# The attention of a two-layer block, one head at a time and two heads at a time

## The reference, cut to what matters

```python
qa, ka = rope(rms_norm(qa)), rope(rms_norm(ka))    # 4 heads of 64
qb, kb = rope(rms_norm(qb)), rope(rms_norm(kb))    # 8 heads of 64 on 2 of k and v
qc, kc = rope(rms_norm(qc)), rope(rms_norm(kc))    # 4 heads, each 2 halves of 32
ya = softmax(causal(qa @ ka.T * 64**-0.5)) @ va
yb = softmax_with_sink(window(qb @ kb.T * 64**-0.5)) @ vb
p = softmax(causal(qc @ kc.T * 32**-0.5))          # for both halves
yc = rms_norm((p[0] - lam * p[1]) @ vc) * (1 - lam_init)
merged = g0 * (ya @ w_pa) + g1 * (yb @ w_pb) + g2 * (yc @ w_pc)
x = x + merged @ w_out
```

## Time and profile before

| | |
|---|---|
| median of 3 runs | 2590.4 us (2590.0 to 2590.89) |
| span of the profiled execution | 2589.5 us |
| PE busy | 2536.0 us, 98% |
| DVE busy | 1838.2 us, 71% |
| ACT busy | 1304.3 us, 50% |
| POOL busy | 116.2 us, 4% |
| DMA, mean over the span | 215 GB/s |

### The profile page before, as it was taken

One profiled execution on the slowest core, in us unless ns is written; L12 is line 12 of the kernel. 1 busy time (PEld: TensorE's weight loads), 2 busy tenths in 40 slices (PEclk: granted clock), 3 DMA queues, 4 the chain that ended last, 5 costly groups with the idle time before them and its releaser, 6 DMA issues.

```text
span 2589.5 us, 41592 instructions
## 1 busy us (share of the span) xinstructions
PE 2536.0 (98%) x16522; PEld 2192.0 (85%) x16522; DVE 1838.2 (71%) x2257; ACT 1304.3 (50%) x1535; POOL 116.2 (4%) x125
## 2 busy tenths in 40 slices
PE   8999999999999999999999999999999999999997
PEld 7888999888999988789989887788888888888886
DVE  6647767855777565375554843698898888988988
ACT  5554545453544421234334212377677677777765
POOL 1100000300000011100000110000000000000000
PEclk9999999999999999999999999899999999999998
DMA  5344553423555331136544212489989999999995
GB/s 213 140 183 159 183 181 145 144 97 134 212 180 195 131 131 66 66 147 235 182 151 164 106 66 98 171 332 357 353 339 354 344 347 358 348 349 344 352 353 211
DMA packets 77326, 558.21 MB, mean 216 GB/s; under 512 B 8704, under 2 KB 8960, under 8 KB 9856
## 3 DMA queue, kind: packets, MB, share of 16 engines
q1 hardware_dynamic: 76320, 550.93, 57.4%
q0 software_dynamic: 864, 5.24, 0.5%
HBM read 555.09 MB, written 1.05 MB: 215 GB/s over the span
## 4 chain that ended last, share of the span: by engine, by line
PE 91%; DVE 4%; ACT 2%; issue 2%; DMA 0%; DVEq 0%; ACTq 0%; SPq 0%; POOL 0%
PE bank L648 23%; PE bank L1137 18%; PE bank L1162 10%; PE bank L638 9%; PE bank L677 7%; PE bank L709 4%; PE bank L729 3%; PE bank L662 2%; PE bank L1110 1%; DVE w_lo L2489 1%; PE bank L1147 1%; PE bank L956 1%; PE bank L970 1%; PE bank L967 1%; ACT w_hi L1645 1%
## 5 line engine op out<-in xcount | busy, mean ns | idle before, releaser
L2489 DVE TENSOR_TENSOR w_lo<-ring,w_hi 128x2048 fp32r<-128x2048 f32 x216 | 486.2, 2288 | 54.1 <-ACT w_hi L1645 53.0
L1645 ACT ACTIVATE w_hi<-ring 128x2048 fp32r<-128x2048 f32 x216 | 404.9, 1916 | 20.6 <-PE bank L1137 17.0
L1137 PE MATMUL bank<-w_hi,xe_hi 128*128 128x512 f32 x792 | 311.4, 393 | 1.1
L1137 PE MATMUL bank<-w_hi,xe_lo 128*128 128x512 f32 x792 | 308.7, 390 | 0.0
L1137 PE MATMUL bank<-w_lo,xe_hi 128*128 128x512 f32 x792 | 308.5, 390 | 0.0
L648 PE MATMUL bank<-x_hi,w_hi 128*128 128x256 f32 x1008 | 285.3, 283 | 0.0
L648 PE MATMUL bank<-x_hi,w_lo 128*128 128x256 f32 x1008 | 285.2, 283 | 0.0
L648 PE MATMUL bank<-x_lo,w_hi 128*128 128x256 f32 x1008 | 285.2, 283 | 0.0
L1740 DVE TENSOR_TENSOR w_lo<-ring,w_hi 128x2048 fp32r<-128x2048 f32 x97 | 222.1, 2290 | 86.5 <-ACT w_hi L1266 84.4
L638 PE MATMUL bank<-xT,ring 128*128 128x256 f32 x1088 | 253.8, 385 | 1.1 <-ACT Z L1554 1.1
L1266 ACT ACTIVATE w_hi<-ring 128x2048 fp32r<-128x2048 f32 x99 | 189.4, 1913 | 109.4 <-PE bank L677 71.4
(11 more groups left out here) (371 smaller groups left out, 5127.4 us busy)
## 6 DMA issues: line engine op xcount, KB each, us to landing
ring<-in_stream SPq DMA_DIRECT2D x431, 1024.0 KB, 5.1
yT<-in_stream SPq DMA_DIRECT2D x54, 1024.0 KB, 6.9
xT<-in_stream SPq DMA_DIRECT2D x27, 1024.0 KB, 7.1
Z<-in_stream SPq DMA_DIRECT2D x8, 1024.0 KB, 8.1
norm_rows<-in_rows POOLq DMA_DIRECT2D x4, 1024.0 KB, 8.5
par<-in_par SPq DMA_DIRECT2D x1, 1335.0 KB, 9.6
cst<-in_cst SPq DMA_DIRECT2D x1, 1216.0 KB, 13.3
xres<-in_x SPq DMA_DIRECT2D x2, 512.0 KB, 4.1
```

Source lines behind the costliest of these rows:

```text
L1137: r = mm(banks[4 + j % 2], a[:, k, :], moe_part(b, i)[:, q * 512:(q + 1) * 512], start=(k == 0 and a is xe_hi and b is w_hi), stop=(k == K ...
L1645: act_(moe_part(w_hi, at), moe_slot(at), ACT.Copy).then_inc(*A.done("moe_hi", at))
L2489: v.tensor_tensor(moe_part(w_lo, at), moe_slot(at), moe_part(w_hi, at).bitcast(F32), ALU.subtract)\
```

## The change

Two jobs of `JOBS` make a pair, and a step now takes a pair: 10 pairs and 13 steps. The two heads of a pair of a or b lie in partitions 0 to 63 and 64 to 127 of q and k; for c the pair is c0 and c1 of one head, in neighbouring 32 partitions. The steps stand after the halves 18, 20, 21, 23, 25, 27, 28, 30, 32, 34, 35, 37 and 39:

```diff
+        PAIRS = [(JOBS[2 * t], JOBS[2 * t + 1]) for t in range(len(JOBS) // 2)]
+        N_PAIRS = len(PAIRS)
...
-            out, steps_left = [], list(range(len(JOBS) + 3))
-
-            def step():
-                if not steps_left:
+            out, steps_left = [], list(range(N_PAIRS + 3))
+
+            def step(halves_done):
+                t = N_PAIRS + 3 - len(steps_left)
+                if not steps_left or halves_done < (3 + 7 * (t - 1) // 4 if t else 1):
                     return
-                t = steps_left.pop(0)
-                if t < len(JOBS):
+                steps_left.pop(0)
+                if t < N_PAIRS:
                     out.append(("score", t))
-                if 1 <= t <= len(JOBS):
+                if 1 <= t <= N_PAIRS:
                     out.append(("norm", t - 1))
-                if 2 <= t <= len(JOBS) + 1:
+                if 2 <= t <= N_PAIRS + 1:
                     out.append(("turn", t - 2))
                 if 3 <= t:
                     out.append(("value", t - 3))
+                if not steps_left:
+                    out.append(("csquare", 0))
...
-                if k >= FIRST_STEP:
-                    step()
+                step(2 * (k - FIRST_STEP) + 1)
                 out.append(("half", 2 * k + 1))
-                if k >= FIRST_STEP:
-                    step()
+                step(2 * (k - FIRST_STEP) + 2)
```

The scores of a pair go to two banks, banks 0 and 1 for even pairs and banks 6 and 7 for odd ones; the latter are those of `sumsq` and `rotate`, so that score 1 waits for their last readers. The matmuls of the two heads alternate. The six transposes of a pair of a or b take bank 2 and 128 columns in each of the two banks of the pair scored a step before:

```diff
+                            if n >= 3 and br_pairs(n - 3):
+                                pe.wait_ge(*A.of("probT", l, n - 3))
+                        elif n == 1:
+                            pe.wait_ge(*A.of("qrms", l, len(QK_PAIRS) - 1))
+                            pe.wait_ge(*V.of("rotsin", l, len(QK_PAIRS) - 1))
+                        for late in range(2):
+                            for bank, (br, h, ot, ob, qt, kt, base, kk_, vc) in zip(score_banks(n), PAIRS[n]):
+                                q = qk[base:base + kk_, qt * SEQ:(qt + 1) * SEQ]
+                                k = qk[base:base + kk_, kt * SEQ:(kt + 1) * SEQ]
+                                if late:
+                                    mm(bank[:, 128:384], q[:, 128:256], k, start=True, stop=True).then_inc(*T.done("score", l, n))
+                                else:
+                                    mm(bank[:, 0:128], q[:, 0:128], k[:, 0:128], start=True, stop=True)
+                    elif kind == "turn":
...
+                            pe.wait_ge(*A.of("probT", l, n - 1))
+                        for j in ((0, 1) if br_pairs(n) else (1,)):
+                            for i in range(3):
+                                at = 3 * j + i if br_pairs(n) else i
+                                r = nc.tensor.transpose(banks[2][:, at * P:(at + 1) * P] if at < 4 else score_banks(n + 1)[at - 4][:, 384:512],
+                                                        prob[:, n % 3, j, cols3(i)], ct("ident"))
```

The values of two heads go to columns 0 to 63 and 64 to 127 of the array, alternating. For c the values of two pairs (two heads) are taken together, with the odd pair:

```diff
+                    elif kind == "value" and values_in(n):
...
+                        if n >= 1:
+                            pe.wait_ge(*A.of("y", l, PAIRS[n - 1][0][2] if br_pairs(n) else PAIRS[n][0][2] - 1))
+                        for late in range(2):
+                            for j in range(2):
+                                br, h, ot, ob, qt, kt, base, kk_, vc = PAIRS[n][j] if br_pairs(n) else PAIRS[n - 1 + j][1]
+                                dst, turned = banks[3][ob:ob + HD, 0:SEQ], probTs[turned_to(n)][:, j * 384:(j + 1) * 384]
+                                if late:
+                                    mm(dst[:, 128:256], vtm[:, 1, vc:vc + HD], turned[:, 256:384], start=False, stop=True)\
+                                        .then_inc(*T.done("value", l, n))
+                                else:
+                                    mm(dst, vtm[:, 0, vc:vc + HD], turned[:, 0:256], start=True, stop=False)
```

with `values_in(t)` giving `[t]` for a and b, and for c `[t - 1, t]` where t is odd, else nothing. So there are 10 scores, 10 turns (6 of six transposes, 4 of three) and 8 values. The mask's result is written to `prob` (three buffers of two heads), and the exponential works in place there; `msk` is gone. ACT:

```diff
+                        nm, rsm, se = sm(f"negmax{n % 2}", 4), sm(f"rowsum{n % 2}", 4), sm(f"sinkexp{n % 2}", 4)
+                        for j in range(2):
+                            for i, s in enumerate((slice(0, 128), slice(128, 384))):
+                                at = 2 * j + i
+                                act_(prob[:, n % 3, j, s], prob[:, n % 3, j, s], ACT.Exp, bias=nm[:, at:at + 1],
+                                     scale=scale, accum_out=rsm[:, at:at + 1]).then_inc(*A.done("exp", l, n))
...
+                        for u in turned_before(n):
+                            sc.wait_ge(*T.of("value", l, u))
+                        to = probTs[turned_to(n)]
+                        if br_pairs(n):
+                            act_(to[:, 0:512], banks[2], ACT.Copy).then_inc(*A.done("probT", l, n))
+                            for j in range(2):
+                                act_(to[:, (4 + j) * P:(5 + j) * P], score_banks(n + 1)[j][:, 384:512], ACT.Copy)\
+                                    .then_inc(*A.done("probT", l, n))
+                        else:
+                            act_(to[:, (n % 2) * 384:(n % 2 + 1) * 384], banks[2][:, 0:384], ACT.Copy).then_inc(*A.done("probT", l, n))
```

On DVE there are four masks in a row and one negative maximum of four columns; one reciprocal of four columns; and, for c, the first half is scaled by the same instruction as a and b and the second subtracted from it:

```diff
-                        if n >= 2:
-                            ve.wait_ge(*A.of("exp", l, n - 2))
-                            ve.wait_ge(*V.of("prob", l, n - 2))
-                        for i, s in enumerate((slice(0, 128), slice(128, 384))):
-                            v.tensor_tensor_reduce(out=msk[:, n % 2, s], in0=banks[n % 2][:, s], in1=mask[:, s], scale=1.0,
-                                                   scalar=-3.0e38, op0=ALU.add, op1=ALU.max,
-                                                   accum_out=sm("rowmax", 2)[:, i:i + 1]).then_inc(*V.done("masked", l, n))
+                        if n >= 3:
+                            ve.wait_ge(*T.of("turnp", l, n - 3))
+                        for j in range(2):
+                            for i, s in enumerate(blocks):
+                                v.tensor_tensor_reduce(out=prob[:, n % 3, j, s], in0=score_banks(n)[j][:, s], in1=mask[:, s], scale=1.0,
+                                                       scalar=-3.0e38, op0=ALU.add, op1=ALU.max,
+                                                       accum_out=sm("rowmax", 4)[:, 2 * j + i:2 * j + i + 1]).then_inc(*V.done("masked", l, n))
...
+                        if br[0] == "c":
+                            v.tensor_scalar(rsm[:, 2:4], rsm[:, 2:4], sm("neglam", 1), None, ALU.mult).then_inc(*V.done("rlam", l, n))
+                        for i, s in enumerate(blocks):
+                            v.tensor_scalar(prob[:, n % 3, 0, s], prob[:, n % 3, 0, s], rsm[:, i:i + 1], None, ALU.mult)\
+                                .then_inc(*V.done("prob", l, n))
+                        if br[0] == "c":
                             own()
-                        for i, s in enumerate((slice(0, 128), slice(128, 384))):
-                            pb = prob[:, n % 3, s]
-                            if br == "c1":
-                                v.scalar_tensor_tensor(out=pb, in0=pb, scalar=rsm[:, i:i + 1],
-                                                       in1=prob[:, (n - 1) % 3, s], op0=ALU.mult, op1=ALU.add)\
-                                    .then_inc(*V.done("prob", l, n))
+                        for i, s in enumerate(blocks):
+                            pb = prob[:, n % 3, 1, s]
+                            if br[0] == "c":
+                                v.scalar_tensor_tensor(out=pb, in0=pb, scalar=rsm[:, 2 + i:3 + i], in1=prob[:, n % 3, 0, s],
+                                                       op0=ALU.mult, op1=ALU.add).then_inc(*V.done("prob", l, n))
```

More of the change, by code:

```diff
@@ L397, in emit, with br_pairs, score_banks, turned_to @@
         SCHED = attention_schedule()
+        def br_pairs(t):
+            return PAIRS[t][0][0] in "ab"
+        def score_banks(t):
+            return (banks[0:2], banks[6:8])[t % 2]
+        def turned_to(t):
+            return t % 2 if br_pairs(t) else t // 2 % 2
+        def values_in(t):
+            return [t] if br_pairs(t) else [t - 1, t] if t % 2 else []
+        def turned_before(t):
+            own = t - t % 2 if not br_pairs(t) else t
+            return [u for u in range(own) if values_in(u) and turned_to(u) == turned_to(t)][-1:]
         class Filler:
@@ L1333, in unit @@
                         act_(squares[:, 8 * SEQ:9 * SEQ], bank[:, 0:SEQ], ACT.Square).then_inc(*A.done("square", l, 8))
-                        act_(msk[:, 0, 0:SEQ], bank[:, SEQ:2 * SEQ], ACT.Copy).then_inc(*A.done("in1", l, n))
+                        act_(vb_rows, bank[:, SEQ:2 * SEQ], ACT.Copy).then_inc(*A.done("in1", l, n))
                     elif n < 9:
@@ L1361, in block1 @@
                             .then_inc(*A.done("vb", l))
+                    if kind == "csquare":
+                        for i in range(2):
+                            sc.wait_ge(*A.of("y", l, 6 + i))
```

(27 more changed lines are left out.)

59 lines of the change are left out of this document (17 added, 42 removed).

## The result

The median went from 2590.89 us (2590.00 to 2591.32, five runs) to **2580.41 us** (2579.42 to 2580.95, five runs): ratio 0.9959, 95% interval 0.9947 to 0.9970, 10.5 us less. The profiled execution of the changed kernel has a span of 2579.1 us against 2589.5.

What follows compares the result with a forecast made beforehand. PE, busy 98% of the span, bounds the kernel; its 17.4 us saving per layer shrinks to 6.9 through waits. Less 3.4 for clock, over two layers, plus 1.5: 8.5 us gained, forecast 2582 us, range 2575 to 2589.

Steps and rivals of the forecast that it cites:

- Pairs at once: PE's scores and values: two heads run together at one head's price plus .03 us; PE saves 17.4 us per layer.
- Rival 2: Scores and values: pairs don't run at once in the array, each costing .60 us more; 2585 us, chance 0.15.
- Score 1's wait: At half 20, PE stands idle at score 1 until DVE's rotsin 6 ends; 5.8 us.
- The ring: After score 1, DVE and ACT's queued masks, exponentials, copies and splits set the pace; 9.1 us per pair of b.
- Rival 1: After score 1, PE keeps its own pace, DVE and ACT not binding; 2564 us, chance 0.1.
- Turn 8: Near the stage's end, PE waits some 3.2 us for pair 9's masks and norm 8; turn 8 at 163.7 us.
- The clock: After the idle at score 1 and turn 8, one low-clock stretch each; 1.7 us each, 3.4 per layer.
- Rival 3: After score 1's wait the low clock lasts, costing 8.5 us per layer instead of 1.7; 2596 us, chance 0.1.
- The projection: After csum, it starts at 185.1 us instead of 192.0 in layer 0, before clock losses; gain 6.9 us per layer.

Runs made afterwards that it cites:

- doubled kernel: Every score and value of a pair multiplied twice on PE into the same place, signalled after the second, against the changed kernel; 2584.23 us.
- copies first: ACT takes the copies of a step's turn and value ahead of that step's exponentials, against the changed kernel; 2565.15 us.
- rotsin ahead: DVE takes rotsin 6 ahead of the split of unit 11, against the changed kernel; 2569.23 us.

## Why the prediction was right

The forecast was 2582 us and 2580.41 came, by the forecast's own mechanism. Point by point:

- **Pairs at once: right.** A pair costs .86 for a score (forecast .88) and .80 for a value (forecast .82). The doubled kernel agrees: a second pass over both heads adds .65 to a score and .65 to a value, what one head's score takes without the .20 of entry (.85). So the two column halves stream entirely at once. The estimate that the prediction drew from the Trainium skill ("TensorE: Matmul & The Clock Gate", section "Measured speedup vs the span model"), .15 more per value, is not what this trace shows: two heads' value takes no longer than one head's. Rival 2 falls.
- **Score 1's wait: right.** 5.72 us (forecast 5.8), ended by rotsin in both layers; moved away by itself, it gave back what it cost.
- **The ring: right.** 61.0 us to the masks of pair 9 (forecast 61.7). The masks stood at 161.8 where 160.4 was forecast ahead of the clock's 1.7. Both "copies first" and "twice" show that it sets the pace. Rival 1 falls. The Trainium skill says in "TensorEngine Tiling (Array Packing)", section "PSUM Bottleneck", that packing doesn't speed up the emptying of PSUM. The trace agrees, as DVE's masks and ACT's copies out of the banks are in the ring; but the exponentials and the splits, which read no bank, are the larger part of its 8.98 us.
- **Turn 8: right time, wrong releaser.** It stood at 165.61; 163.7 and 1.7 of clock are 165.4. But the prediction's step "PE waits for the masks and norm 8" failed: norm 8 was over by 164.8, and the copy of turn 7 behind the exponentials of pair 9 ended last. PE was there at 161.5, earlier than 160.5 + 1.7, so it stood for 4.1 rather than 3.2. Turn 8 came 3.8 us behind the masks of pair 9 where 3.3 was reckoned, and the masks came .3 early, so the time of turn 8 is close partly by luck.
- **The clock: right behind which waits, wrong in length.** One stretch of 3.4 us was taken for each; behind score 1 it was 6.8, in both layers. Part of that fell while PE still stood: it went on at 93.71 and full clock came at 98.2. Score 1 with half 21 then took 5.9 (93.71 to 99.62), where .85 and 3.04 at full clock are 3.9: 2.0 us lost. Behind turn 8 it was 1.5: from turn 8 to turn 9 it took 8.55, and 7.01 in "rotsin ahead", whose layer 0 has full clock there. That makes 3.5 per layer where 3.4 was forecast, so the sum is right by luck: one stretch was longer and cost little more, the other cost less. Rival 3 falls: no stretch at 0.50 in a stage of the changed kernel lasted over 6.8 us.
- **The projection: right.** 187.8 against 185.1 + 3.4 = 188.5, so the gain was 4.2 and 6.0 where 3.5 and 5.0 were reckoned. That .7 and 1.0 make up the 1.6 us by which the time is better than forecast.

What stays open is why the clock fell for 6.8 us behind score 1 and for 3.4 behind turn 8, and for only 3.4 at score 1 in layer 0 of the doubled kernel, after 5.08 us of idle time; and why layer 1 sometimes has a stretch that layer 0, with the same waits, has not.

## What to carry to other kernels

When PE's work is packed tighter, what comes next is the order in the queues of the engines behind it: follow one round through the in-order queues of DVE and ACT, and add the durations, even if each engine is half idle. In such a queue put first what another engine waits for and whose operands are there (the copy that empties a bank, the one rotation that opens a bank), and last what can only start later. Give a step its place by when its operand is ready, not as early as the order allows, for waits of 2 to 6 us here sometimes also cost 1.5 to 2.0 us of clock behind them.

## What was not expected of the hardware

- Two heads ran at once even when their matmuls weren't neighbours in the program: both of one head's, then both of the other's, cost the same .86 us, with starts 12 to 14 ns apart, and the second head's first product ahead of the first head's second.
- Two column halves with all 128 rows under them streamed at twice the rate of one, as quarters of 64 rows did in the earlier trace rows: both heads' value took .80 us, as one head's before, and a second pass of both .65 us more.
- After 5.72 us without work PE's clock was at 0.50 for 6.8 us, 4.5 of it (93.71 to 98.20) with PE back at work, where 2.08 us of idle time was followed by 3.3 and the same 2 us at turn 0 of "rotsin ahead" by none in layer 0 and by some 3 us in layer 1.
